# Feed-forward stages in groups of two f: four units' high products, then their low products, then two down units

## Chip, cores and metric

The kernel runs on one core of a Trainium2 chip. The metric is the device time of one execution in microseconds (us), the median of several runs. Lower is better.

## What is computed

The reference is four transformer blocks in a row on 256 tokens of width 1024, all in fp32. Each block has two SwiGLU feed-forward halves, so there are eight of them in all:

```python
def swiglu_ffn(x, wi, wo):
    g, u = jnp.split(x @ wi, 2, axis=-1)
    return (jax.nn.silu(g) * u) @ wo
...
x = x + 0.5 * swiglu_ffn(rmsnorm(x, ffn1_norm[i]), ffn1_wi[i], ffn1_wo[i])
```

The inner width is 2816, which is 22 slices of 128; a slice is called f. Between the feed-forward halves lie mixers (a chunked recurrence and windowed attention in the first two blocks; convolution, pooling and differential attention in the last two) and, in the first two blocks, a gate. The change doesn't touch these.

## The kernel before

**Weights.** All weights stream once through the core in units of 128 x 1024 fp32 (512 KB). SyncE loads unit u into one of four raw buffers as soon as the low part of unit u-4 is done. ScalarE then writes the high part of the unit, rounded to fp32r (`split` of `scalar`, L1190; it waits until the unit that had the slot before has been used up), and VectorE the low part, raw minus high (`split` of `vector`, L1821). High and low part of a unit share one of five slots (`W_SLOTS`), handed out to whichever was used longest ago (`placed_units`, L309). `step(s, k)` on ScalarE and VectorE makes the parts of the unit that lies three places ahead of place k of the stage (`lead`, L334; in the two feed-forward stages ahead of a `mixer2` the lead grows by one at each of k = 48, 51 and 54, as more slots are lent).

**A feed-forward stage** has 66 units, in the order of `ffn_order` (L60): two gate-and-up units per f (`gu`, each with half of the 1024 inputs), and one down unit per f (`o`). Each `gu` unit has eight high products with 512 columns (`gate_up_high`, L499: weights' high part against high and low part of x, side by side) and eight low products with 256 columns (`gate_up_low`, L518: weights' low part against x's high part). A slice uses two PSUM banks, 4 and 5 or 6 and 7 in turn. The order is two high units, their two low parts, one down unit (that of f-3), and so on. A down unit has twelve products of 512 columns (`unit_job`, L402).

**Between gate and down.** VectorE sums the halves of both banks (`summed`, L1956, two reductions), scales (`gated`, L1966), ScalarE applies Silu, VectorE multiplies (`product`, L1972), ScalarE rounds to the high part (`high_h`, L1261), VectorE subtracts (`low_h`, L1980). A down unit waits for `low_h` of its f. ScalarE and VectorE work through their instructions in program order, so these small operations stand in one queue with the splits.

**Stage ends.** The last two down units are worked together in `tail` (L451), by four blocks of the output; ahead of the last block TensorE transposes the first half of the new x (`turn_x`, L437). Those transposes wait for the first two additions of `into_x` (L1937) on VectorE, which stand in VectorE's queue behind the splits of the next stage's first units. In the very last stage `end_tail` (L472) works the last three down units together. At a stage's start `rest` transposes the other half of x.

Of the kernel before, what the change touches and what calls it, by code (L numbers as in the profile page):

```python
# [14 lines left out]
P = 128  # L15
# [29 lines left out]
TURNED_STEPS = ((0, 6), (8, 6))  # L45
# [108 lines left out]
def program(nc, d, out):  # L154
    ctx = ExitStack()
    with ctx:
# [237 lines left out]
        def tensor(pe, w):  # L394
# [103 lines left out]
            def ffn(s, n, m, u0):  # L498
# [52 lines left out]
                for k, (kind, f, half) in enumerate(ffn_order()):  # L551
# [3 lines left out]
                    if k == 6 and n != 11:  # L555
                        turn_r()
# [7 lines left out]
                    if kind == "gu":  # L564
                        gate_up_high(u, f, half)
                        if (n, k) == (11, 6):
# [617 lines left out]
        def scalar(act, w):  # L1184
# [70 lines left out]
            def ffn(s, i, n, m, u0):  # L1255
# [9 lines left out]
                order = ffn_order()  # L1265
                for k, (kind, f, half) in enumerate(order):
                    u = u0 + k
                    if u > 0 and (n, k) not in TURNED_STEPS:
                        step(s, k)
                    if k == 1 and n:  # L1270
                        rest(n)
                    if k == 2 and n in (0, 11):
                        squares(n)
                    if (n, k) == (0, 5):
                        w.wait_ge(*at("brow"))
                        copy(bias_row, pb[0][0:8, 0:384]).then_inc(*up("brow_out"))
                    if k == 6:
                        w.wait_ge(*at("rt", n))
                        copy(sbuf_h[:, 0, 1, :], pb[3][:, 0:S]).then_inc(*up("rrow", n))
                        for g in range(3):  # L1280
                            silu(g)
                        for g in range(2):
                            high_h(g)
                        if (n, k) in TURNED_STEPS:
                            step(s, k)
                    elif k > 6 and order[k - 1][2] == 1:
                        g = order[k - 1][1]
                        silu(g)
                        if g == NF - 1:
                            high_h(g)  # L1290
                        if g == 12 and n == 8:
                            w.wait_ge(*at("windows"))
                            copy(Pg[:, :, :, :], part2("tap").rearrange("p (g s t) -> p g s t", g=4, s=2)).then_inc(*up("Pg"))
                        if g == 4 and n in (2, 6):
                            w.wait_ge(*at("pin", i))
                            copy(PTh[:, :, :], pin).then_inc(*up("ph", i))
                    elif k > 6 and order[k - 2][2] == 1 and order[k - 2][1] < NF - 1:
                        high_h(order[k - 2][1])
# [487 lines left out]
            split(2)  # L1786
            for c in range(4, 8):
                high_x(0, c)
            split(3)
# [30 lines left out]
        def vector(dve, w):  # L1820
# [132 lines left out]
            def ffn(s, i, n, m, u0):  # L1953
                r_rows = sbuf_h[:, 0, 1, :]

                def summed(f):  # L1956

                    b = 4 + 2 * (f % 2)
                    w.wait_ge(*at("used", u0 + order.index(("gu", f, 1))))
# [25 lines left out]
                order = ffn_order()  # L1985
                for k, (kind, f, half) in enumerate(order):
                    u = u0 + k
                    if (n, k) in ((11, 2), (0, 2), (0, 3)):
                        summed(f)
# [1163 lines left out]
```

## Time and profile before

| | |
|---|---|
| median of 3 runs | 2049.31 us (2049.3 to 2049.9) |
| profiled execution: its own time | 2048.94 us |
| span of its trace | 2047.1 us |
| TensorE busy (matmuls) | 2038.7 us, 100% of the span |
| VectorE busy | 1488.5 us, 73% |
| ScalarE busy | 1097.2 us, 54% |
| HBM read | 375.73 MB, 184 GB/s |
| mean granted TensorE clock | 0.999 |

PE is TensorE's matmuls, PEld its weight loads, DVE VectorE, ACT ScalarE. In a timeline each row has the start in us, the time from start to end in us, the engine, the line, the operation, what it writes and reads, the shape and how many instructions were merged; in brackets the idle time before it and who ended that. Ends of matmuls are modelled and they overlap, so the pace of TensorE is read from start to start. L1188 is ScalarE's `copy`, used for splits (128x1024) and for `high_h` (128x256) alike.

### The profile page before, as it was taken

To read this page: it belongs to the slowest core of one execution; us is meant where nothing else is said; L and a number is where in the kernel's file an instruction comes from. 1 tells how busy PE (TensorE), PEld (TensorE's weight loads), DVE (VectorE), ACT (ScalarE), POOL (GpSimd) and SP (SyncE) were. 2 spreads that over 40 slices of the span, in tenths; PEclk is the share of its full clock that TensorE was granted. 3 is DMA by queue.
4 is the path that set the end of the run, shared out by engine and by line. 5 is a ranking of instruction groups with operands and counts; after the bars stand their busy time and mean duration, and the time that the engine had idled before them with its cause. 6 is when DMAs were issued, how large, how long until landed. Compare 5 with 4: busy or idle time off the path is not lost.

```text
span 2047.1 us, 27834 instructions
## 1 busy us (share of the span) xinstructions
PE 2038.7 (100%) x10803; PEld 1744.2 (85%) x10803; DVE 1488.5 (73%) x2240; ACT 1097.2 (54%) x1644; POOL 128.3 (6%) x140
## 2 busy tenths in 40 slices
PE   9999999999999999999999999999999999999998
PEld 8888888888888888888888888888888888888887
DVE  7776677777777767777777777788767777788766
ACT  5444664544554456655445545685445545685444
POOL 1000100000000001000000000160000000160000
PEclk9999999999999999999999999999999999999999
DMA  8654545555555555455555756425565656525553
GB/s 260 198 189 163 195 154 199 185 187 186 189 192 189 185 174 176 154 195 196 190 186 183 250 184 224 167 94 198 193 195 188 204 194 215 167 94 198 192 193 126
DMA packets 105539, 378.82 MB, mean 185 GB/s; under 512 B 12173, under 2 KB 12837, under 8 KB 105152
## 3 DMA queue, kind: packets, MB, share of 16 engines
q1 hardware_dynamic: 102224, 368.16, 53.9%
q0 software_dynamic: 2208, 7.71, 1.2%
q8 instruction: 86, 1.41, 0.3%
q10 hardware_dynamic: 976, 1.17, 0.2%
q14 instruction: 45, 0.37, 0.1%
HBM read 375.73 MB, written 1.27 MB: 184 GB/s over the span
## 4 chain that ended last, share of the span: by engine, by line
PE 99%; DVE 0%; DMA 0%; issue 0%; ACT 0%; ACTq 0%; POOLq 0%; POOL 0%
PE pb L516 31%; PE pb L527 16%; PE pb L415 15%; PE pb L416 14%; PE pb L420 14%; PE pb L586 1%; PE pb L443 1%; PE pb L463 1%; PE pb L465 1%; PE pb L464 1%; PE pb L989 0%; PE pb L650 0%; DMA X<-in_x 0%; PE pb L679 0%; PE pb L1030 0%
## 5 line engine op out<-in xcount | busy, mean ns | idle before, releaser
L1188 ACT ACTIVATE whi<-raw 128x1024 fp32r<-128x1024 f32 (+1 forms) x684 | 708.3, 1045 | 534.7 <-PE pb L527 421.1
L1827 DVE TENSOR_TENSOR wlo<-raw,whi 128x1024 fp32r<-128x1024 f32 (+1 forms) x680 | 821.8, 1217 | 46.9 <-ACT whi L1188 46.8
L516 PE MATMUL pb<-XT,whi 128*128 128x512 f32 x2784 | 665.8, 390 | 0.8 <-DVE XT L1842 0.5
L516 PEld LDWEIGHTS pb<-XT,whi 128*128 128x128 f32 x2784 | 519.6, 188 | 108.0 <-issue 1.5
L527 PEld LDWEIGHTS pb<-XT,wlo 128*128 128x128 f32 x2784 | 359.1, 191 | 14.9
L527 PE MATMUL pb<-XT,wlo 128*128 128x256 f32 x2784 | 363.9, 283 | 0.0
L1963 DVE TENSOR_REDUCE sbuf_s<-pb 128x256 f32<-128x512 f32 x240 | 154.6, 686 | 229.8 <-PE pb L527 229.8
L415 PE MATMUL pb<-whi,HTh 128*128 128x512 f32 x796 | 313.4, 394 | 0.1
L416 PE MATMUL pb<-whi,HTl 128*128 128x512 f32 x796 | 311.6, 391 | 0.0
L420 PE MATMUL pb<-wlo,HTh 128*128 128x512 f32 x796 | 302.1, 389 | 0.0
L420 PEld LDWEIGHTS pb<-wlo,HTh 128*128 128x128 f32 x796 | 149.5, 188 | 32.5
L415 PEld LDWEIGHTS pb<-whi,HTh 128*128 128x128 f32 x796 | 150.1, 189 | 26.9 <-issue 0.2
L416 PEld LDWEIGHTS pb<-whi,HTl 128*128 128x128 f32 x796 | 150.1, 189 | 24.9
L415 PE MATMUL pb<-whi,XT 128*128 128x512 f32 (+2 forms) x448 | 169.5, 382 | 0.0
L416 PE MATMUL pb<-whi,XT 128*128 128x512 f32 (+2 forms) x448 | 166.3, 375 | 0.0
L1963 DVE TENSOR_REDUCE sums<-pb 128x256 f32<-128x512 f32 x112 | 72.2, 686 | 127.9 <-PE pb L527 127.9
L2785 POOL TENSOR_TENSOR st<-st,cst 128x2 f32<-128x2 f32 (+3 forms) x35 | 49.8, 1423 | 1710.3 <-DVE st L1853 1516.2
L1259 ACT ACTIVATE sbuf_s<-sbuf_s 128x256 f32<-128x256 f32 x120 | 49.6, 419 | 168.4 <-DVE sbuf_s L1970 168.4
L420 PE MATMUL pb<-wlo,XT 128*128 128x512 f32 (+2 forms) x448 | 134.0, 375 | 0.0
L415 PEld LDWEIGHTS pb<-whi,XT 128*128 128x128 f32 x448 | 84.2, 188 | 16.3 <-issue 1.7
L416 PEld LDWEIGHTS pb<-whi,XT 128*128 128x128 f32 x448 | 84.4, 188 | 14.2
L420 PEld LDWEIGHTS pb<-wlo,XT 128*128 128x128 f32 x448 | 81.4, 188 | 15.4
(262 smaller groups left out, 1596.8 us busy)
## 6 DMA issues: line engine op xcount, KB each, us to landing
raw<-in_W SPq DMA_DIRECT2D x694, 512.0 KB, 4.2
raw<-in_W SPq DMA_DIRECT2D x8, 264.0 KB, 2.9
scr<-in_bc POOLq DMA_DIRECT2D x2, 640.0 KB, 5.1
raw<-in_W SPq DMA_DIRECT2D x4, 256.0 KB, 6.0
scr<-scratch POOLq DMA_DIRECT2D x8, 128.0 KB, 4.7
scr<-mrow POOLq DMA_DIRECT2D x2, 512.0 KB, 5.1
scr<-in_slope POOLq DMA_DIRECT2D x1, 1024.0 KB, 11.0
scr<-in_Pg POOLq DMA_DIRECT2D x1, 1024.0 KB, 14.2
```

Of the source, the lines that this page charges most:

```text
L415: pe.matmul(o, ah, bh, start=begin and i == 0, stop=False)
L416: pe.matmul(o, al, bh, start=False, stop=False)
L420: ins = pe.matmul(o, ah, bl, start=False, stop=end and i == len(parts) - 1)
L443: ins = pe.transpose(pb[b][:, t * P:(t + 1) * P], X[:, t, c * P:(c + 1) * P], ident[:, :])
L463: pe.matmul(o, ah, h[:, n * 512:n * 512 + 512], start=False, stop=False)
L516: pe.matmul(pb[b + j][:, :], h[:, k:k + P], xs, start=c == 0, stop=False)
L527: ins = pe.matmul(pb[b + j][:, 0:S], l[:, k:k + P], XT[:, c, 0, :], start=False, stop=c == KD - 1)
L1188: return act.activation(o, i, ACT.Copy, scale=scale)
L1259: act.activation(g, g, ACT.Silu).then_inc(*up("silu", s, f))
L1827: dve.tensor_tensor(low_w(u)[:, 0:c], raw[u % RAW_SLOTS][:, 0:c], high_w(u)[:, 0:c].bitcast(F32), ALU.subtract).then_inc(*up("lo", u))
L1963: dve.tensor_reduce(sums_of(f)[:, j, :], pb[b + j][:, :].rearrange("p (s t) -> p t s", s=2), AXX, ALU.add).then_inc(*up(name, s, f))
L2785: pool.tensor_tensor(r, v, cst[:, 0:1].to_broadcast([P, n]), ALU.pow).then_inc(*done)
```

## The change

A stage now goes in groups of two f. For f and f+1 the four `gu` units' high products come first, then their low products, then the down units of f-2 and f-1. The first four units do the same (their low products in the order 0, 2, 1, 3); for the last two f the low products follow after each f's two high units, as before. ScalarE's and VectorE's programs of the stage are written out anew for that order; the two exceptions named in `TURNED_STEPS` go. In the kernel's opening `split(2)` moves behind the four `high_x` (on VectorE `low_x`) calls. No work is added or left out.

```diff
 def ffn_order():
     order = [("gu", 0, 0), ("gu", 1, 0), ("gu", 0, 1), ("gu", 1, 1)]
-    for f in range(2, NF):
-        order += [("gu", f, 0), ("gu", f, 1)]
-        if f > 2:
-            order.append(("o", f - 3, 0))
-    return order + [("o", f, 0) for f in range(NF - 3, NF)]
+    for f in range(2, NF, 2):
+        order += [("gu", f, 0), ("gu", f, 1), ("gu", f + 1, 0), ("gu", f + 1, 1), ("o", f - 2, 0), ("o", f - 1, 0)]
+    return order + [("o", f, 0) for f in range(NF - 2, NF)]
+
+def low_products(k):
+    if k == 3:
+        return (0, 2, 1, 3)
+    kind, f, half = ffn_order()[k]
+    if k < 4 or kind == "o" or half == 0:
+        return ()
+    if f >= NF - 2:
+        return (k - 1, k)
+    return (k - 3, k - 2, k - 1, k) if f % 2 else ()
...
                         gate_up_high(u, f, half)
-                        if f < 2:
-                            gate_up_low(u, f, half)
-                        elif half == 1:
-                            gate_up_low(u - 1, f, 0)
-                            gate_up_low(u, f, 1)
+                        for q in low_products(k):
+                            _, g, part = order[q]
+                            gate_up_low(u0 + q, g, part)
...
 # ScalarE, one group
+                for f in range(2, NF - 2, 2):
+                    k = 3 * f - 2
+                    if f > 2:
+                        step(s, k)
+                        step(s, k + 1)
+                    step(s, k + 2)
+                    step(s, k + 3)
+                    silu(f)
...
+                    step(s, k + 4)
+                    silu(f + 1)
+                    high_h(f)
+                    if f == 12 and n == 8:
+                        w.wait_ge(*at("windows"))
+                        copy(Pg[:, :, :, :], part2("tap").rearrange("p (g s t) -> p g s t", g=4, s=2)).then_inc(*up("Pg"))
+                    step(s, k + 5)
+                    high_h(f + 1)
+                f = NF - 2
+                k = 3 * f - 2
+                step(s, k)
+                step(s, k + 1)
+                step(s, k + 2)
+                silu(f)
+                step(s, k + 3)
+                high_h(f)
+                step(s, k + 4)
+                silu(f + 1)
+                high_h(f + 1)
+                for q in range(k + 5, k + 8):
+                    step(s, q)
...
             split_half(1, 0)
             split_half(1, 1)
-            split(2)
             for c in range(4, 8):
                 high_x(0, c)
+            split(2)
             split(3)
...
 # VectorE, one group
+                for f in range(2, NF - 2, 2):
+                    k = 3 * f - 2
+                    if f > 2:
+                        step_and_lambda(k)
+                        low_h(f - 1)
+                        step_and_lambda(k + 1)
+                    step_and_lambda(k + 2)
+                    summed(f)
+                    step_and_lambda(k + 3)
+                    gated(f)
+                    summed(f + 1)
+                    step_and_lambda(k + 4)
+                    gated(f + 1)
+                    product(f)
...
+                    step_and_lambda(k + 5)
+                    product(f + 1)
+                    low_h(f)
+                f = NF - 2
+                k = 3 * f - 2
+                step(s, k)
+                low_h(f - 1)
+                step(s, k + 1)
+                summed(f)
+                step(s, k + 2)
+                gated(f)
+                step(s, k + 3)
+                product(f)
+                summed(f + 1)
+                gated(f + 1)
+                step(s, k + 4)
+                low_h(f)
+                product(f + 1)
+                low_h(f + 1)
+                for q in range(k + 5, k + 8):
+                    step(s, q)
```

## Rows read from the trace of the kernel before

**Rows 1.** The profile's page: span, TensorE's busy time, chain of work.
```profile
span 2047.1 us, 27834 instructions
...
PE 2038.7 (100%) x10803; PEld 1744.2 (85%) x10803; DVE 1488.5 (73%) x2240; ACT 1097.2 (54%) x1644; POOL 128.3 (6%) x140
...
PE 99%; DVE 0%; DMA 0%; issue 0%; ACT 0%; ACTq 0%; POOLq 0%; POOL 0%
```

**Rows 2.** Timeline of TensorE in the second feed-forward stage, one f and the next.
```profile
510.28 3.79 PE L516 MATMUL pb<-XT,whi 128*128 128x512 f32 x16
513.91 2.08 PE L527 MATMUL pb<-XT,wlo 128*128 128x256 f32 x16
515.82 0.40 PE L415 MATMUL pb<-whi,HTh 128*128 128x512 f32 x1
...
518.57 3.79 PE L516 MATMUL pb<-XT,whi 128*128 128x512 f32 x16
```

**Rows 3.** Timeline of VectorE and ScalarE in the same f.
```profile
515.12 1.06 ACT L1188 ACTIVATE whi<-raw 128x1024 fp32r<-128x1024 f32 x1 [2.89 <-PE pb L527]
...
516.02 1.29 DVE L1963 TENSOR_REDUCE sums<-pb 128x256 f32<-128x512 f32 x2 [2.53 <-PE pb L527]
517.23 0.41 DVE L1970 TENSOR_TENSOR sums<-sums,sbuf_h 128x256 f32<-128x256 f32 x1
517.56 1.22 DVE L1827 TENSOR_TENSOR wlo<-raw,whi 128x1024 fp32r<-128x1024 f32 x1
518.70 0.42 DVE L1977 TENSOR_TENSOR sbuf_h<-sums 128x256 f32<-128x256 f32 x1
...
517.68 0.42 ACT L1259 ACTIVATE sums<-sums 128x256 f32<-128x256 f32 x1 [1.49 <-DVE sums L1970]
518.00 1.04 ACT L1188 ACTIVATE whi<-raw 128x1024 fp32r<-128x1024 f32 x1
```

**Rows 4.** Timeline at the same stage's end: VectorE, ScalarE, then TensorE's tail and transposes.
```profile
526.98 0.42 DVE L1977 TENSOR_TENSOR sbuf_h<-sbuf_s 128x256 f32<-128x256 f32 x1
...
528.84 3.50 DVE L1827 TENSOR_TENSOR wlo<-raw,whi 128x1024 fp32r<-128x1024 f32 x3 [0.52 <-ACT whi L1188]
532.25 1.41 DVE L1842 SCALAR_TENSOR_TENSOR X<-pb,st,X 128x512 f32<-128x512 f32 x2
...
527.43 0.42 ACT L1188 ACTIVATE HTh<-sbuf_h 128x256 fp32r<-128x256 f32 x1 [1.05 <-DVE sbuf_h L1977]
527.76 3.14 ACT L1188 ACTIVATE whi<-raw 128x1024 fp32r<-128x1024 f32 x3
...
529.58 0.39 PE L463 MATMUL pb<-whi,HTh 128*128 128x512 f32 x1
...
533.66 1.03 PE L443 MATMUL pb<-ident,X 128*128 128x128 f32 x8
```

**Rows 5.** Timeline of the kernel's opening: TensorE, then ScalarE.
```profile
10.17 1.11 PE L527 MATMUL pb<-XT,wlo 128*128 128x256 f32 x8
11.12 1.09 PE L516 MATMUL pb<-XT,whi 128*128 128x512 f32 x4
12.05 1.03 PE L443 MATMUL pb<-ident,X 128*128 128x128 f32 x8
...
13.85 1.10 PE L527 MATMUL pb<-XT,wlo 128*128 128x256 f32 x8
...
11.33 1.06 ACT L1188 ACTIVATE whi<-raw 128x1024 fp32r<-128x1024 f32 x1 [0.64 <-DMA raw<-in_W]
12.47 1.57 ACT L1188 ACTIVATE XT<-pb,gcol 128x256 fp32r<-128x256 f32 x4
```

**Rows 6.** Timeline at the start of the stage behind the second gate (n = 8).
```profile
1120.94 1.98 PE L516 MATMUL pb<-XT,whi 128*128 128x512 f32 x8
...
1122.59 0.69 DVE L2472 TENSOR_TENSOR X<-X,scr 128x512 f32<-128x512 f32 x1
```

**Rows 7.** Timeline of ScalarE: the one copy of `Pg`, in the stage n = 8.
```profile
1221.06 1.90 ACT L1188 ACTIVATE Pg<-scr 128x2048 fp32r<-128x2048 f32 x1
```

More of the change, by code:

```diff
@@ L549, in end_ready @@
                     w.wait_ge(*at("hl", s, NF - 3 + i))
-                for k, (kind, f, half) in enumerate(ffn_order()):
+                order = ffn_order()
+                for k, (kind, f, half) in enumerate(order):
                     u = u0 + k
@@ L554, in ffn @@
                         rest(n)
-                    if k == 6 and n != 11:
+                    if k == 7 and n != 11:
                         turn_r()
@@ L1263, in high_h @@
                     copy(HTh[:, f % H_SLOTS, :], sbuf_h[:, f % 2, 0, :]).then_inc(*up("hh", s, f))
[L1265 to L1268, printed above, removed]
-                        step(s, k)
[L1270 to L1298, printed above, removed]
@@ new lines, in ffn @@
+                if u0:
+                    step(s, 0)
+                step(s, 1)
+                if n:
+                    rest(n)
+                if n in (0, 11):
+                    squares(n)
+                for k in range(2, 6):
+                    step(s, k)
+                if n == 0:
+                    w.wait_ge(*at("brow"))
+                    copy(bias_row, pb[0][0:8, 0:384]).then_inc(*up("brow_out"))
+                w.wait_ge(*at("rt", n))
+                copy(sbuf_h[:, 0, 1, :], pb[3][:, 0:S]).then_inc(*up("rrow", n))
@@ L1958, in summed @@
                     b = 4 + 2 * (f % 2)
-                    w.wait_ge(*at("used", u0 + order.index(("gu", f, 1))))
+                    w.wait_ge(*at("used", u0 + ffn_order().index(("gu", f, 1))))
                     if f > 2:
@@ L2033, in ffn, with step_and_lambda @@
+                def step_and_lambda(k):
+                    step(s, k)
                     if n in (8, 11) and k == 30:
@@ L2036, in ffn @@
                         lam_sum(i)
+                if u0:
+                    step(s, 0)
+                step(s, 1)
+                if n:
+                    rest(n)
+                summed(0)
+                if n in (0, 11):
+                    mean_x(n)
+                step(s, 2)
+                summed(1)
+                step(s, 3)
+                step(s, 4)
+                w.wait_ge(*at("r", n))
+                dve.tensor_copy(sbuf_h[:, 1, 1, :].rearrange("p (t e) -> p t e", t=2),
+                                r_of(n).unsqueeze(2).to_broadcast([P, 2, P])).then_inc(*up("rcopy", n))
@@ new lines, in ffn @@
+                dve.tensor_scalar(half_r(n), r_of(n), 0.5, None, ALU.mult).then_inc(*up("hr", n))
+                step(s, 5)
+                gated(0)
+                gated(1)
+                product(0)
+                product(1)
+                low_h(0)
+                low_h(1)
+                for f in range(2, NF - 2, 2):
[12 more added lines that the diff above has]
+                    product(f)
+                    if f == 4 and n in (2, 6):
+                        w.wait_ge(*at("ph", i))
+                        dve.tensor_tensor(PTl[:, :, :], pin, PTh[:, :, :].bitcast(F32), ALU.subtract).then_inc(
+                            *up("pl", i))
+                    step_and_lambda(k + 5)
+                    product(f + 1)
+                    low_h(f)
@@ new lines, in ffn @@
+                f = NF - 2
+                k = 3 * f - 2
+                step(s, k)
+                low_h(f - 1)
[13 more added lines that the diff above has]
+                    step(s, q)
@@ L2037, in ffn @@
+                u = u0 + len(ffn_order()) - 1
                 w.wait_ge(*at("hr", n))
@@ L2745, in vector @@
             split_half(1, 1)
-            split(2)
             for c in range(4, 8):
                 low_x(0, c)
+            split(2)
             split(3)
```

58 lines of the change are left out of this document (8 added, 50 removed).

## The prediction

> **What bounds the kernel now.** I read the page first: TensorE is busy for 2038.7 of 2047.1 us, and the chain that ended last is TensorE for 99% [rows 1]. So only two things can move the time: the pace of the matmuls, or pauses of TensorE that are there now or come new.
>
> For the pace I read TensorE's timeline in the middle of a feed-forward stage [rows 2]. From 510.28 to 513.91 it does 16 high products, 3.63 us or 227 ns each; to 515.82 16 low ones, 1.91 us or 119 ns each; to 518.57 the 12 products of a down unit, 2.75 us or 229 ns each. One f takes 8.29 us, with no pause: each change from one kind to the next comes at the pace of the kind that ends. In units: H (high products of one unit) 1.815, L (low) 0.955, O (down) 2.755.
>
> Then I read what the other two engines do in that time [rows 3]. ScalarE's split begins at 515.12, 1.21 us after the L that frees its slot began, having waited 2.89 us for it; VectorE's sums begin at 516.02, 2.11 us after the first L, having waited 2.53 us. Neither engine is late for anything. From start to start VectorE takes 1.21 for a pair of sums, 0.33 for a small operation and 1.14 for a split; ScalarE 0.32 for a Silu. A handover between them costs 0.04 (gated ends at 517.64, Silu starts at 517.68), a split of ScalarE 1.05, or 0.95 where the next instruction is ready.
>
> **The change, part by part.** The number of matmuls, splits, sums and loads stays the same, so the edit is worth nothing on TensorE by itself. Switches between high and low products become fewer, and a switch costs nothing now [rows 2]. What it can do is make TensorE wait.
>
> *A group in steady run.* TensorE's group is 4 H, 4 L, 2 O: 7.26 + 3.82 + 5.51 = 16.59, twice 8.29. Count from its first H and call its units 0 to 5. Slots come free in a burst: unit 0's at 7.26 + 1.21 = 8.47 for ScalarE, then 9.43, 10.38, 11.34. With five slots, unit 5 goes into the slot of unit 0, unit 6 into that of unit 1, and so on; so a chain through the two queues starts at 8.47. In program order: split 5, 8.47 to 9.52; its low part on VectorE, 9.56 to 10.70; sums of f to 11.91; low part 6 to 13.05; gated 13.47; Silu 13.50 to 13.82; split 7 to 14.87; low part 7, 14.91 to 16.05; gated of f+1 to 16.38; product of f to 16.80; its high part 16.83 to 17.15; split 8 to 18.20; low part 8, 18.24 to 19.38; product of f+1 to 19.80; its high part to 20.15; split 9 to 21.20. Unit 9 is the fourth H of the next group and is wanted at 16.59 + 5.45 = 22.03. So it comes 0.8 ahead. The others are earlier still (unit 8: 18.20 against 20.22; the down units and the high and low parts of f by several us). In steady run I take zero pauses, with 0.8 us of cover; the cover is gone if the chain of 12.7 us is 7% longer.
>
> *A stage's end.* Here the chain's lateness counts. The last group's program goes H H L L H H L L O O tail, with the tail at 16.59 again. ScalarE comes out of the group before at 20.15 - 16.59 = 3.57. Then: splits 61, 62, 63 to 4.62, 5.57, 6.52; VectorE low part 61, 4.66 to 5.80; low of f = 19 to 6.13; low part 62 to 7.27; sums of f = 20 to 8.48; low part 63 to 9.62; gated 10.04; Silu to 10.39; split 64 to 11.44; low part 64, 11.48 to 12.62; product 20 to 13.04; sums of f = 21, 12.96 to 14.17; gated 14.50; low part 65 to 15.64; low of 20 to 15.98 (done 16.06); product 21, 15.98 to 16.40. Before, that last product stood at 526.98, 2.60 ahead of the tail at 529.58 [rows 4]; now 0.6 ahead. Behind it in program order stand its high part, three splits on ScalarE (the next stage's first units), their three low parts on VectorE, and then the two additions into x. Before, these additions ran from 532.25 to 533.66, and TensorE's transposes began at 533.66: no slack at all [rows 4]. By the same steps they now run from 21.26 to 22.67, which is 4.67 behind the tail's start and not 2.67. So TensorE stands before the transposes, 2.0 us per stage end. (The low part of f = 21, done at 17.30, makes a pause of 0.1 in the tail, which is inside the 2.0.) The cost is read from no row directly: its lower bound is 0, if VectorE comes to the additions in time; the upper 3.1, with one more split in the chain. I take 2.0, since each step is a row.
>
> That upper case is the rule in the two stages ahead of the last mixers: there the lead grows at k = 54, which puts one split more into the group f = 18, and all that follows comes 1.14 later (one low part). 3.1 each. In the very last stage nothing is queued behind, but `end_tail` wants the low part of f = 20 at 11.08 + 2.755 + 1.36 = 15.2 and gets it at 16.06: 0.9.
>
> *The kernel's opening.* TensorE's second unit may start at 10.17 now, when the first H ends, and takes the same 2.73 (11.12 to 13.85, with eight transposes) [rows 5]: done at 12.90. The third H wants split 2. ScalarE's four `high_x` follow the transposes by 0.42 (12.05 to 12.47), so they now start near 11.5 and take 1.57; split 2, which ran ahead of them at 11.33, then ends at 14.05 [rows 5]. A pause of 1.2 that the low products used to fill. From 0 (if split 2 came first again) to 1.5.
>
> *Stages behind a gate* (n = 4 and 8). The second half of x is complete at 1123.28 [rows 6]. The transposes that want it come one H after the stage's start now, 1122.75, and not an H and an L after it: 0.5, and 0.1 for the first of them to be split. 0.6 each, 0 to 0.8. Other stages' additions end earlier; zero.
>
> *The copy of Pg.* It takes 1.90 [rows 7] and stands now ahead of split 8 in the chain: 0.8 of cover goes, 1.1 is a pause. Before it had TensorE's slack. 0 to 1.9.
>
> Sum: five stage ends at 2.0 are 10.0; two at 3.1 are 6.2; the last 0.9; opening 1.2; gates 1.2; Pg 1.1. Together 20.6. The profiled execution took 2048.94 with a span of 2047.1; 2048.94 + 20.6 = 2069.5. The median lies 0.4 above that execution, so 2070 us.
>
> **The rivals.** *One: the steady chain doesn't fit.* If handovers cost more than 0.04 where several waits meet, all 9 hand-overs from group to group in 8 stages pause. The point is 0.8 us more on the chain; at 0.3 us beyond it the price is 72 x 0.3 = 22, so 2092. For: the chain crosses the engines twelve times. Against: rows 3 show these crossings with their waits, at 0.04.
>
> *Two, not slower: the additions are in time.* At seven stage ends VectorE reaches the additions within 2.7 us of the tail's start, as now. This decides if the chain out of the group before is 2 us shorter than I have it, for instance if splits 61 to 63 run early. Then 16.2 and the 0.9 drop out, and 2070 becomes 2053, which is within 0.2%. For it: nothing is recomputed, both engines have idle time. Against: program order holds each split behind a Silu or a high part.
>
> *Three, faster: longer batches run at a better pace.* Eight low products take 0.95 (10.17 to 11.12), 16 take 1.91: 119 ns each in both [rows 5, 2]. Reading to 0.01 us, doubling the batch can save at most some 1 ns each; on 2816 low products that is 3 us, so even without any pause 2046. The Trainium skill (Perfetto Trace Analysis, Matmul Optimizations) says that TensorE scales power with its utilization and that it is therefore important to run matmuls back-to-back in batches. By that rule this change is a gain; the rows bear none of it out, as they stand back-to-back now.
>
> **How the numbers follow.** Forecast 0.65; rival one 0.18; two 0.13; three 0.04. A measurement of this kernel can tell 0.2%, 4 us, from no change. Faster by more than that: rival three with luck, 0.03. Within: rival two and the rest of three, 0.10, as half an us more at some stage end carries rival two out. Slower: 0.87. The range: the forecast's own terms run from 2060 (stage ends at 1.0, opening and gates at half) to 2082 (all stage ends at 3.1, Pg 1.9). Towards rival two I go to 2055, towards rival one to 2090; beyond them lie some 2 in 10.
>
> **What would show it.** Right: TensorE without pause from group to group; at each stage end the transposes (L443) begin 2 us later after the tail's first product (L463) than the 4.08 us of now [rows 4], named as waiting for VectorE's L1842; the third H of the opening waiting for ScalarE's split. Wrong: a pause ahead of every fourth H, named as ScalarE's split; or transposes in time at the stage ends; or another pace than 227 and 119 ns.

## The result, and the profile after

The changed kernel takes 2069.8 us (median of four runs, 2069.19 to 2070.36); the kernel before took 2049.61 us beside it (2049.3 to 2049.92). The ratio is 1.0098, 95% interval 1.0086 to 1.011: 20.2 us slower. The forecast was 2070. The profiled execution took 2070.36 us with a span of 2068.5, 21.4 above the span of before.

The page of the changed kernel, which answers to [rows 1]. In it L525 are the high products, L536 the low ones, L424, L425 and L429 the down units, L472 to L474 the tail, L452 transposes of x, L489 `end_tail`; L1196 is ScalarE's copy, L1851 VectorE's low parts, L1866 among others its additions into x.

```profile
span 2068.5 us, 27833 instructions
...
PE 2043.0 (99%) x10803; PEld 1741.5 (84%) x10803; DVE 1492.7 (72%) x2240; ACT 1085.4 (52%) x1644; POOL 127.1 (6%) x140
...
PE 89%; DVE 6%; ACT 3%; issue 2%; DMA 1%; SPq 0%; POOLq 0%; POOL 0%; ACTq 0%; DVEq 0%
```

TensorE does the same 10803 products, and the chain that ended last was TensorE's for 99% of the span; now it is for 89%, and VectorE and ScalarE stand in it with 9%. So it is no longer only its own pace that TensorE follows. For whom it waits, the view of its waits tells (what waited, for whom: us in total, times, longest):

```profile
PE pb L452 <- DVE X L1866: 9.3, 14, 1.1
PE pb L525 <- ACT whi L1196: 2.5, 3, 1.0
PE pb L472 <- DVE HTl L2006: 2.4, 4, 1.0
PE pb L525 <- DVE XT L1866: 1.8, 2, 1.1
...
PE pb L489 <- DVE HTl L2006: 0.8, 1, 0.8
```

The first line is the stage ends: 14 waits, two at each of seven ends, of transposes for the additions into x. One of these ends, that of the second feed-forward stage, in the timeline: TensorE, then VectorE, then ScalarE. It answers to [rows 4].

```profile
533.24 0.39 PE L472 MATMUL pb<-whi,HTh 128*128 128x512 f32 x1
...
537.28 0.39 PE L474 MATMUL pb<-whi,HTl 128*128 128x512 f32 x1
538.75 0.30 PE L452 MATMUL pb<-ident,X 128*128 128x128 f32 x1 [1.08 <-DVE X L1866]
539.32 0.98 PE L452 MATMUL pb<-ident,X 128*128 128x128 f32 x7 [0.27 <-DVE X L1866]
...
528.12 1.23 DVE L1851 TENSOR_TENSOR wlo<-raw,whi 128x1024 fp32r<-128x1024 f32 x1 [1.43 <-ACT whi L1196]
...
532.60 0.41 DVE L2001 TENSOR_TENSOR sbuf_h<-sbuf_s 128x256 f32<-128x256 f32 x1
...
534.44 3.50 DVE L1851 TENSOR_TENSOR wlo<-raw,whi 128x1024 fp32r<-128x1024 f32 x3 [0.52 <-ACT whi L1196]
537.86 2.06 DVE L1866 SCALAR_TENSOR_TENSOR X<-pb,st,X 128x512 f32<-128x512 f32 x3
...
526.72 0.42 ACT L1267 ACTIVATE sums<-sums 128x256 f32<-128x256 f32 x1 [3.53 <-DVE sums L1994]
527.04 1.04 ACT L1196 ACTIVATE whi<-raw 128x1024 fp32r<-128x1024 f32 x1
```

The additions begin at 537.86, 4.62 behind the tail's first product at 533.24; before, it was 532.25 - 529.58 = 2.67. The transposes follow with two pauses. Further up stands where VectorE lost time: from 526.69 to 528.12 it did nothing, since the next thing in its program is the low part of a unit whose high part ScalarE makes only after Silu (526.72, then the split at 527.04).

Below, n numbers the parts of the program in order: the feed-forward stages are n = 0, 2, 4, 6, 8, 10, 11 and 13; a gate stands ahead of n = 4 and 8, a `mixer2` behind n = 8 and 11. An end with neither a `mixer2` nor the kernel's end behind it (n = 0, 2, 4, 6, 10) is called a plain end. Laying both traces over each other at the same products of TensorE, the lag of the changed kernel grows like this (us):

| place | predicted | measured |
|---|---|---|
| opening (first stage up to its tail) | 1.2 | 1.85 |
| five plain stage ends | 5 x 2.0 | 1.95, 1.95, 1.96, 1.96, 1.94 |
| gate ahead of n = 4 | 0.6 | 0.59 |
| n = 8: gate, Pg, end | 0.6 + 1.1 + 3.1 = 4.8 | 5.21 |
| n = 11: a pause, end | 3.1 | 3.72 |
| last stage: its `end_tail` | 0.9 | 1.07 |
| steady run of the stages n = 2, 6, 10 and 13, and the mixers | 0 | -0.73 |
| sum | 20.6 | 21.5 |

### The profile page after: what moved, and what is told of

Read it like the earlier page. It is cut to its first block, busy times and chain, and to the rows that moved or that the text cites. A ratio compares the mean times of both kernels' runs of the same rounds, so it can differ in the third digit from the quotient of the medians.

```text
span 2068.5 us, 27833 instructions
## 1 busy us (share of the span) xinstructions
PE 2043.0 (99%) x10803; PEld 1741.5 (84%) x10803; DVE 1492.7 (72%) x2240; ACT 1085.4 (52%) x1644; POOL 127.1 (6%) x140
## 3 DMA queue, kind: packets, MB, share of 16 engines
q10 hardware_dynamic: 976, 1.17, 0.2%
## 4 chain that ended last, share of the span: by engine, by line
PE 89%; DVE 6%; ACT 3%; issue 2%; DMA 1%; SPq 0%; POOLq 0%; POOL 0%; ACTq 0%; DVEq 0%
PE pb L525 29%; PE pb L536 15%; PE pb L424 13%; PE pb L425 13%; PE pb L429 13%; DVE wlo L1851 2%; ACT whi L1196 2%; PE pb L594 1%; PE pb L452 1%; DMA raw<-in_W 1%; DVE sbuf_s L1987 1%; PE pb L474 1%; PE pb L472 1%; PE pb L473 1%; DVE X L1866 0%
## 5 line engine op out<-in xcount | busy, mean ns | idle before, releaser
L1851 DVE TENSOR_TENSOR wlo<-raw,whi 128x1024 fp32r<-128x1024 f32 (+1 forms) x680 | 820.9, 1216 | 384.9 <-ACT whi L1196 384.7
L1196 ACT ACTIVATE whi<-raw 128x1024 fp32r<-128x1024 f32 (+1 forms) x684 | 692.2, 1044 | 310.9 <-PE pb L536 202.3
L525 PE MATMUL pb<-XT,whi 128*128 128x512 f32 x2768 | 650.0, 390 | 4.4 <-ACT whi L1196 2.5
L525 PEld LDWEIGHTS pb<-XT,whi 128*128 128x128 f32 x2768 | 516.8, 188 | 114.1 <-ACT whi L1196 6.6
L536 PEld LDWEIGHTS pb<-XT,wlo 128*128 128x128 f32 x2768 | 344.4, 191 | 7.2
L536 PE MATMUL pb<-XT,wlo 128*128 128x256 f32 x2768 | 347.1, 283 | 0.0
L424 PE MATMUL pb<-whi,HTh 128*128 128x512 f32 x804 | 315.6, 392 | 0.0
L425 PE MATMUL pb<-whi,HTl 128*128 128x512 f32 x804 | 313.9, 390 | 0.0
L429 PE MATMUL pb<-wlo,HTh 128*128 128x512 f32 x804 | 305.2, 389 | 0.0
L429 PEld LDWEIGHTS pb<-wlo,HTh 128*128 128x128 f32 x804 | 151.0, 188 | 32.2
L424 PEld LDWEIGHTS pb<-whi,HTh 128*128 128x128 f32 x804 | 151.3, 188 | 28.8
L425 PEld LDWEIGHTS pb<-whi,HTl 128*128 128x128 f32 x804 | 151.3, 188 | 27.8
L424 PE MATMUL pb<-whi,XT 128*128 128x512 f32 (+2 forms) x448 | 169.6, 382 | 0.0
L425 PE MATMUL pb<-whi,XT 128*128 128x512 f32 (+2 forms) x448 | 166.2, 375 | 0.0
L1196 ACT ACTIVATE HTh<-sbuf_h 128x256 fp32r<-128x256 f32 x176 | 73.3, 418 | 143.3 <-DVE sbuf_h L2001 143.3
L429 PE MATMUL pb<-wlo,XT 128*128 128x512 f32 (+2 forms) x448 | 134.0, 375 | 0.0
L424 PEld LDWEIGHTS pb<-whi,XT 128*128 128x128 f32 x448 | 84.2, 188 | 16.3 <-issue 1.7
L1267 ACT ACTIVATE sums<-sums 128x256 f32<-128x256 f32 x56 | 23.5, 419 | 139.1 <-DVE sums L1994 139.1
L425 PEld LDWEIGHTS pb<-whi,XT 128*128 128x128 f32 x448 | 84.4, 188 | 14.2
```

The costliest lines, as they stand in the source:

```text
L424: pe.matmul(o, ah, bh, start=begin and i == 0, stop=False)
L425: pe.matmul(o, al, bh, start=False, stop=False)
L429: ins = pe.matmul(o, ah, bl, start=False, stop=end and i == len(parts) - 1)
L525: pe.matmul(pb[b + j][:, :], h[:, k:k + P], xs, start=c == 0, stop=False)
L536: ins = pe.matmul(pb[b + j][:, 0:S], l[:, k:k + P], XT[:, c, 0, :], start=False, stop=c == KD - 1)
L1196: return act.activation(o, i, ACT.Copy, scale=scale)
```

## The experiments

Each undoes a part, adds a known load, or changes one order. Line numbers shift by a few between kernels. "Lag" is counted as in the table.

**Is there really no slack at a stage's end?** Kernel before, with two subtractions of 128x512 (0.69 us each) into a scrap tile on VectorE, ahead of the last low part of each stage; nothing reads the scrap.

```diff
             def step(s, k):
                 for u in split_at(s, k):
+                    if stages[s][0] == "ffn" and k == 65 and u < n_units:
+                        w.wait_ge(*at("hi", u))
+                        for cut in (slice(0, 512), slice(512, 1024)):
...
+                            dve.tensor_tensor(pad[:, :], raw[u % RAW_SLOTS][:, cut], high_w(u)[:, cut].bitcast(F32),
+                                              ALU.subtract).then_inc(*up("pad", s, cut.start))
                     split(u)
```

> The kernel before, with two further subtractions of 128 x 512 on VectorE (into a scrap tile; some 1.3 us together) ahead of the last low part at each of seven stage ends. Theory (no slack between the additions and the transposes): each end grows by 1.3, 2049.5 + 9 = 2058.5. Rival (the transposes were in time with room to spare, and the pause of the changed kernel has another cause): 2049.5 to 2051.

Measured: 2058.49 us (ratio 1.0045, 1.0029 to 1.0062). Two of them, back to back, take 1.33 from start to start (532.25 to 533.58); the lag over an end is 1.24 to 1.34 at six of the seven (1.87 at n = 11). All of it reaches the end: no slack, as the prediction read from [rows 4]. VectorE, then TensorE's tail, at the end of the second stage:

```profile
532.25 1.41 DVE L1848 TENSOR_TENSOR pad<-raw,whi 128x512 bf16<-128x512 f32 x2
533.58 1.22 DVE L1828 TENSOR_TENSOR wlo<-raw,whi 128x1024 fp32r<-128x1024 f32 x1
534.72 1.40 DVE L1853 SCALAR_TENSOR_TENSOR X<-pb,st,X 128x512 f32<-128x512 f32 x2
...
530.72 0.39 PE L464 MATMUL pb<-whi,HTh 128*128 128x512 f32 x1
```

**Does the steady chain have its 0.8 us of cover?** Changed kernel with scrap copies on ScalarE, right ahead of the split that stands behind Silu of f, in each group from f = 4 on; in one kernel one copy of 128x512 (0.61 us), in the other two of 128x1024 (1.05 us each).

```diff
                     silu(f)
...
+                    for j in range(1 if f > 2 else 0):
+                        w.wait_ge(*at("ss", *in_junk[-1]))
+                        in_junk.append((n, "pad", (f, j)))
+                        copy(junk[:, 0:512], X[:, 0, 0:512]).then_inc(*up("ss", *in_junk[-1]))
                     step(s, k + 4)
```

> The changed kernel with one further ScalarE copy of 128 x 512 (into a scrap tile, some 0.6 us) ahead of the Silu of f+1 in each group from f = 4 on, so that the chain through the two queues is 0.6 longer. Theory (0.8 us of cover in steady run, none at the stage ends): no pause from group to group, 0.5 to 0.6 more at each of eight ends, 2074. Rival (the steady chain has no cover): 56 further pauses of 0.5, 2098 or more.

> As before, with two copies of 128 x 1024, some 2.0 us on the chain. Theory (0.8 us of cover): a pause of 1.2 ahead of the fourth high unit of 56 groups, 67 us, and 2.0 at each of eight ends, 16 us: 2153. Rival (the chain doesn't bind, TensorE's lead is larger): as the six tenths of the shorter one, stage ends alone, 2086.

Measured: 2076.93 us (ratio 1.0134) with the small copy, 2173.89 us (a single execution) with the two large ones. TensorE's waits for splits, first of the kernel with one copy, then of the one with two:

```profile
PE pb L525 <- ACT whi L1196: 3.5, 5, 1.0
```
```profile
PE pb L525 <- ACT whi L1196: 50.1, 61, 1.8
```

With 0.6 us more the high products wait for splits at 5 places only (3 in the changed kernel), and between 480 and 520 us TensorE has no pause at all. By the starts of the products one group in n = 2 and one in n = 6 has its fourth high unit 0.28 us late, which this view doesn't list; in the group before it ScalarE has one more copy of 128x512 (`PTh`, 0.61 us), so that there the chain is longer by both. With 2.1 more they wait at 61 places: from group to group. So the cover lies between these two, as worked out.

Both kernels came out slower than expected, by 3 and by 21 us, and the starts of the products tell where. With the small copy the five plain ends cost 0.53 more each, as expected; what came on top stands in the groups of n = 2 and 6 (0.41 each), n = 8 (0.97) and n = 11 (0.31), and at the end of n = 11 (0.7). With the large ones the fourth high unit of a group begins 17.97 behind that of the group before, in place of 16.55. That is 1.42 for each such group, near the 2.1 - 0.8 = 1.3 of the sum, so beyond its cover the chain costs what it overhangs; 56 of them make 80 us, where the expectation took 1.2 each, 67. The plain ends cost 2.05 more each, as expected, but those of n = 8, n = 11 and the last stage 3.7, 4.3 and 4.8. Why these three cost more is not shown.

**Is it the place of the additions in VectorE's queue?** Changed kernel with the first two additions ahead of the last two low parts.

```diff
-                for q in range(k + 5, k + 8):
-                    step(s, q)
+                step(s, k + 5)
...
+                def last_splits():
+                    step(s, k + 6)
+                    step(s, k + 7)
+
+                into_x(u, [hr[:, t:t + 1] for t in range(2)], m, last_splits)
```

> The changed kernel, but at each stage end VectorE makes the first two additions into x ahead of the low parts of the last two of the next stage's first three units, not behind them. Theory (TensorE stands because VectorE's queue reaches the additions late): the additions start about 2.4 us behind the tail's first product and not 4.6, the transposes come in time, and 1.7 us go at each of seven ends: 2069.8 - 11.8 = 2058. Rival (the late product of the last f, not the place of the additions, holds the end, or the additions wait for TensorE's own blocks): the transposes stay late, 2067 to 2070.

Measured: 2064.31 us (ratio 1.0072), 6 off the expectation. The wait of the transposes for the additions (L1866) is gone from the list, but other waits came. The list, then VectorE at the end of the second stage, where the tail's first product begins at 532.22:

```profile
PE pb L424 <- DVE XT L1866: 2.5, 4, 0.6
PE pb L525 <- DVE XT L1866: 2.1, 3, 1.0
```
```profile
534.58 1.54 DVE L1866 SCALAR_TENSOR_TENSOR X<-pb,st,X 128x512 f32<-128x512 f32 x2
536.04 2.35 DVE L1851 TENSOR_TENSOR wlo<-raw,whi 128x1024 fp32r<-128x1024 f32 x2
```

The first two additions are in time, 2.36 behind the tail. But the two low parts that were passed now stand ahead of the remaining additions and of what follows from them, and the next stage's first products wait instead. A plain end cost 0.75 or 1.37 in place of 1.95. So VectorE's queue as a whole is late there, and this order of its last steps passes part of the lateness on; the expectation had left that out.

**Opening and gates.** Changed kernel with the low products of the first four units of each stage right behind their high ones, as before.

```diff
 def low_products(k):
-    if k == 3:
-        return (0, 2, 1, 3)
+    if k < 4:
+        return (k,)
     kind, f, half = ffn_order()[k]
-    if k < 4 or kind == "o" or half == 0:
+    if kind == "o" or half == 0:
         return ()
```

> The changed kernel, but the first four units of each stage have their low products right behind their high ones, as in the kernel before. Theory (in the opening and behind a gate TensorE runs through its high products and then waits for x or a split; low products in between fill that wait): 1.2 goes in the opening and 0.6 at each of two gates: 2069.8 - 2.4 = 2067.4. Rival (the opening waits for its loads whatever the order): 2069 or more.

Measured: 2068.33 us. Against the changed kernel the opening gives back 1.68 us and the two gates 0.72 and 0.65: at these three places the low products had lain over a wait, as the prediction says. But n = 11 became 0.89 slower and the end of n = 0 by 0.27, so the order that the change gave the first four units is the better one there; what waits in those two places I did not follow.

**Pg and the last stage.** Changed kernel with the copy of `Pg` ahead of Silu of its group, and `low_h` of f = 20 ahead of `gated` of f = 21. ScalarE first, then VectorE:

```diff
                     step(s, k + 3)
+                    if f == 12 and n == 8:
+                        w.wait_ge(*at("windows"))
+                        copy(Pg[:, :, :, :], part2("tap").rearrange("p (g s t) -> p g s t", g=4, s=2)).then_inc(*up("Pg"))
                     silu(f)
...
                 summed(f + 1)
+                low_h(f)
                 gated(f + 1)
                 step(s, k + 4)
-                low_h(f)
                 product(f + 1)
```

> The changed kernel with two moves that are apart in time: ScalarE's copy of Pg goes ahead of the Silu of its group, where ScalarE idles 3 us, and at a stage's end the low part of h of f = 20 comes ahead of the last f's scaling. Theory: the pause of 1.0 in the group f = 14 of n = 8 goes, and that of 0.95 in the very last stage: 2069.8 - 1.9 = 2067.9; the other stage ends stay as they are. Rival (these pauses belong to the order of the products, not to two places in the queues): 2069.8.

Measured: 2067.91 us. The sum came out as expected, its parts did not. The stage n = 8 up to its tail gained 2.26 us and n = 11 gained 1.18, the ends of n = 0, 8 and 11 lost 0.64, 0.94 and 0.64, and the last stage kept 0.92 of its 1.07. Of the 2.26 at n = 8, 1.17 lie before the stage's last high product and are the copy of `Pg`, near the 1.1 predicted. The other 1.09 lie right ahead of the tail, like the 1.18 of n = 11, where there is no copy: in the changed kernel the tail waits there for `low_h` (L472 in the list of waits above). The early `low_h` ends that wait but makes VectorE's additions later, 6.03 and 5.64 behind the tail at these two ends in place of 5.03, and it doesn't cure the last stage's pause (the splits do, below).

**All three together.** The three edits above in one kernel.

> The changed kernel with the three edits together: additions ahead of the last two splits, low products right behind the high ones in each stage's first four units, and the copy of Pg and the low part of f = 20 moved up. TensorE's groups of four, four and two stay. Theory (all that the change costs lies in places of the two queues, none in the grouping): 11.8 + 2.4 + 1.9 go, 2053.7; what stays is 1.2 in each of the two tails ahead of the last mixers and 0.8 in n = 11. Rival (the grouping has a price of its own): 2058 or more.

Measured: 2061.51 us (ratio 1.0057), 8 above the expectation. By its number alone the rival of that run, a price of the grouped order itself, would hold. What it left was waits by name (those of the first edit above, and two in the tails, 2.2 us), so the next theory was about who makes VectorE late.

**Who makes VectorE late?** The rows of the stage end say: VectorE stood 1.43 us before a low part whose split was queued on ScalarE behind Silu, which itself waited 3.53 for VectorE. Three kernels from the changed one, VectorE's program being left as it was in the first two. One moves these splits ahead of Silu and the high parts in all groups (and the copy of `Pg` behind Silu of f), the next in the last group alone:

```diff
                     step(s, k + 2)
                     step(s, k + 3)
+                    step(s, k + 4)
+                    step(s, k + 5)
                     silu(f)
...
-                    step(s, k + 4)
                     silu(f + 1)
                     high_h(f)
...
-                    step(s, k + 5)
                     high_h(f + 1)
                 f = NF - 2
...
                 step(s, k + 2)
-                silu(f)
                 step(s, k + 3)
-                high_h(f)
+                silu(f)
                 step(s, k + 4)
+                high_h(f)
                 silu(f + 1)
```

The third has beside these the low products behind the high ones in the first four units of n = 0, 4 and 8 only, and the early `low_h` of f = 20.

```diff
-def low_products(k):
+def low_products(k, n):
+    if k < 4 and n in (0, 4, 8):
+        return (k,)
     if k == 3:
         return (0, 2, 1, 3)
```

> The changed kernel with another order on ScalarE alone: in every steady group the last two splits stand ahead of Silu of f (the copy of Pg behind that Silu), and in the last group the two splits that stood behind Silu and the first high part stand ahead of them. VectorE's program is as it was. The theory says that the lateness at the stage ends grows where VectorE stands 1.43 us before a split that is queued behind Silu or a high part: then the pauses of 2.0 us at five ends and of 3.4 at two, the 0.95 in the last stage, the 1.0 of Pg and the 0.8 of n = 11 go, and 2050 to 2051 us are left (opening 1.7 and two gates at 0.6, less 0.14 in each of eight stages). The rival, that VectorE's own queue of low parts, sums and products is too long for this order whatever ScalarE does, gives 2060 us or more.

> The changed kernel with ScalarE's order changed in the last group of each stage alone (two splits ahead of Silu and the first high part). If the waits of VectorE for splits in that last group make the lateness, 1.43 us go at each of seven ends and 0.95 in the last stage: 2059 us. If the group before it has made it already, about as the changed kernel, 2068 to 2070 us.

> As the kernel with the splits ahead, and beside it the low products of a stage's first four units right behind the high ones in the stages n = 0, 4 and 8 alone (the opening and the two behind a gate), and low of f = 20 ahead of its neighbour's scaling. If opening and gates are then as in the kernel before, 1.7 and 1.2 us more go: 2048.5 to 2049.5 us, level with the kernel before or up to 1 us under it. The rival, that the grouped order keeps a price of its own, gives 2052 us or more.

Measured: 2052.77 us with the splits ahead everywhere (ratio 1.0013, 1.0004 to 1.0023), 2057.93 with them ahead in the last group alone (1.0038, 1.0024 to 1.0052), 2049.9 with the two repairs (1.0000, 0.9991 to 1.0009), which is 0.4 above its expectation. The order of a few instructions on ScalarE, in the last group alone, takes back 12 of 20 us. A plain end gives back 1.5 of its 1.95; at the two ends ahead of a `mixer2` the additions still begin 4.82 and 4.12 behind the tail. With the splits ahead everywhere the pauses of the last stage and of n = 11 are gone too. TensorE's waits, splits ahead everywhere; the transposes' wait of 9.3 us for the additions (L1866) is no longer among them:

```profile
PE pb L525 <- DVE XT L1866: 1.4, 2, 1.1
PE pb L525 <- ACT whi L1196: 1.0, 1, 1.0
PE pb L1172 <- POOL sbuf_s L2965: 1.0, 1, 1.0
PE pb L452 <- DVE X L2514: 0.6, 2, 0.3
```

The kernel with the splits ahead everywhere came out 2 us above the expectation, because the ends were not quite in time: 0.33 to 0.35 at each of five, 0.29 and 0.17 at the two ahead of a mixer2, 2.2 in sum. VectorE and TensorE at the end of the second stage, first of this kernel, then of the one with the splits ahead in the last group alone:

```profile
529.46 0.42 DVE L2001 TENSOR_TENSOR sbuf_h<-sbuf_s 128x256 f32<-128x256 f32 x1
...
534.73 2.06 DVE L1866 SCALAR_TENSOR_TENSOR X<-pb,st,X 128x512 f32<-128x512 f32 x3
...
531.72 0.39 PE L472 MATMUL pb<-whi,HTh 128*128 128x512 f32 x1
...
535.80 1.37 PE L452 MATMUL pb<-ident,X 128*128 128x128 f32 x8
536.92 0.47 PE L472 MATMUL pb<-whi,HTh 128*128 128x512 f32 x1
```
```profile
534.46 2.06 DVE L1866 SCALAR_TENSOR_TENSOR X<-pb,st,X 128x512 f32<-128x512 f32 x3
...
531.35 0.39 PE L472 MATMUL pb<-whi,HTh 128*128 128x512 f32 x1
```

With the splits ahead everywhere the additions begin 3.01 behind the tail, 0.34 more than before's 2.67, and the transposes take 1.12 to the next product, where they took 0.79 before (533.66 to 534.45).

**A version at or under the kernel before.** The last of these kernels with two moves on VectorE in the last group: the last product (of f = 21) goes ahead of the low part that stood before it, and `low_h` of f = 20 goes back behind `gated`, where the changed kernel has it. The expectation names the first move alone; what each of the two is worth is not shown.

```diff
                 summed(f + 1)
-                low_h(f)
                 gated(f + 1)
-                step(s, k + 4)
+                low_h(f)
                 product(f + 1)
+                step(s, k + 4)
                 low_h(f + 1)
```

> As the kernel with the splits ahead and the two small repairs, and beside it VectorE's last product (of f = 21) ahead of the low part that stood before it in the last group. The trace of that kernel still has its additions 0.3 to 0.4 us later behind the tail than the kernel before, at each of five ends, and 0.1 to 0.2 at the two ahead of a mixer2. If the additions are in time now, these 2.1 us go and only the gain of 0.14 us in each stage is left: 2047.6 to 2048.3 us, some 0.08% under the kernel before. If TensorE's pauses there have another cause, 2049.9 us as without it.

Measured: 2047.76 us against 2049.55 of before beside it, ratio 0.9991 (0.9982 to 1.0000); the span is 2045.6 against 2047.1. The grouped order, with its queues in the right order, is not slower, and by this measure 0.09% faster, at the edge of what the interval can tell. At the end of the second stage:

```profile
532.19 1.40 DVE L1868 SCALAR_TENSOR_TENSOR X<-pb,st,X 128x512 f32<-128x512 f32 x2
...
529.69 0.39 PE L474 MATMUL pb<-whi,HTh 128*128 128x512 f32 x1
...
533.78 1.03 PE L454 MATMUL pb<-ident,X 128*128 128x128 f32 x8
534.57 0.48 PE L474 MATMUL pb<-whi,HTh 128*128 128x512 f32 x1
```

Five kernels agree in what an end costs. For the end of n = 2, where "late" is the start of the additions behind the tail's first product, less the 2.67 of before:

| kernel | additions behind tail | late | lag gained over the end |
|---|---|---|---|
| before, with two subtractions | 534.72 - 530.72 = 4.00 | 1.33 | 1.30 |
| changed | 537.86 - 533.24 = 4.62 | 1.95 | 1.95 |
| splits ahead in the last group | 534.46 - 531.35 = 3.11 | 0.44 | 0.45 |
| splits ahead everywhere | 534.73 - 531.72 = 3.01 | 0.34 | 0.33 |
| and the last product ahead | 532.19 - 529.69 = 2.50 | -0.17 | 0.01 |

The kernel with the additions ahead stands outside this: there they come 2.36 behind the tail, in time, and this end still costs 0.75, for the work that they passed.

**What is the small gain in the steady stages?** The stages n = 2, 6, 10 and 13 (up to its `end_tail`) became 0.14 us shorter, which the prediction didn't have. Start to start, the first five wide products (512 columns) behind low ones take 233, 236, 228, 232 and 231 ns, all others 226.7 (means of 18 units in the second stage of before; the same in the changed kernel). That is 27 ns for each such change. The first low products behind wide ones take 113 and 119 ns in place of 120: 7 ns back. My first thought was VectorE's sums, which read the banks just then. To tell the two apart, a kernel from before with the low products of each unit right behind its own high ones:

```diff
-                        if f < 2:
-                            gate_up_low(u, f, half)
-                        elif half == 1:
-                            gate_up_low(u - 1, f, 0)
-                            gate_up_low(u, f, 1)
+                        gate_up_low(u, f, half)
```

> The kernel before with the low products of every gate-and-up unit right behind its own high ones: two changes from high to low and two from low to wider products for each f, in place of one and one. Same products, same work of the other engines. If the first five wide products behind low ones cost 27 ns in sum, and the change from wide to low gives 7 ns back, as the start-to-start times of TensorE's rows say, 20 ns come on top for each of 20 f in 8 stages: 3.2 us, 2052.9 us. The rival is that those products are slow since VectorE's sums read the banks beside them: then nothing is added, 2049.7 us.

Measured: 2052.54 us (ratio 1.0015, 1.0006 to 1.0023). The timeline of TensorE, one f:

```profile
486.27 1.98 PE L516 MATMUL pb<-XT,whi 128*128 128x512 f32 x8
488.09 1.11 PE L527 MATMUL pb<-XT,wlo 128*128 128x256 f32 x8
489.04 2.00 PE L516 MATMUL pb<-XT,whi 128*128 128x512 f32 x8
490.88 1.11 PE L527 MATMUL pb<-XT,wlo 128*128 128x256 f32 x8
491.83 0.40 PE L415 MATMUL pb<-whi,HTh 128*128 128x512 f32 x1
```

Eight high products behind a down unit take 1.82 (486.27 to 488.09), behind low ones 1.84 (489.04 to 490.88), with no sums beside them. Each steady stage became 0.40 us longer, which is 20 times 20 ns. The change of kind is the cause; VectorE's sums are not. In the changed kernel 18 f in nine groups have nine such changes fewer, 0.18 us at 20 ns; the stage gained 0.14, and what takes the rest is not shown.

## Why the prediction was right

*The number.* 2070 against 2069.8 is closer than the working deserves. In the profiled executions the lag is 21.5 and not 20.6, and the terms missed by 0.65 (opening), 1.2 (the ends ahead of a `mixer2`, Pg and the last stage), -0.24 (the plain ends) and -0.73 (steady run and mixers). That these nearly cancel is luck; the mechanism at the stage ends, 10 of the 20 us, is not. The upper end of the forecast's own terms was added wrongly: eight ends at 3.1, 1.9 for Pg, 1.5 for the opening and 1.6 for the gates make 2079, not 2082, which changes nothing in the range.

*What bounds the kernel.* Right. Nothing was added to or taken from TensorE's work, and all that was lost is pauses.

*A group in steady run.* Right in its result and in its steps. The sum put the split of the next group's fourth unit at 20.15 to 21.20 behind the group's first high product. In the trace ScalarE reaches it, after the high part of f+1, like this (ScalarE, then on TensorE the low products of the group that wants the unit):

```profile
486.81 0.42 ACT L1196 ACTIVATE HTh<-sbuf_h 128x256 fp32r<-128x256 f32 x1 [1.62 <-DVE sbuf_h L2001]
487.14 1.99 ACT L1196 ACTIVATE whi<-raw 128x1024 fp32r<-128x1024 f32 x2
...
490.81 4.00 PE L536 MATMUL pb<-XT,wlo 128*128 128x256 f32 x32
```

The group that wants this unit has its low products at 490.81 and so began 7.26 earlier, at 483.55; its fourth unit is wanted 5.45 later, at 489.00. The split began at 487.14, and at 1.04 it ends at 488.18, with 0.8 to spare. Rival one, the chain that doesn't fit, fell: it needed 0.8 us more, and the kernel with 0.6 us more still ran from group to group without pauses, but for those groups where ScalarE had another copy to make.

*A stage's end.* Right: 1.94 to 1.96 for each of the five, where the steps gave 2.0; the additions stood 4.62 behind the tail, where they gave 4.67. The sign that was named came in part: in the second stage the first of the eight transposes begins 5.51 behind the tail and the others 6.08, where before all began 4.08 behind it, so they are 1.43 and 2.0 later, and they wait for the additions (L1866, L1842 of before). Rival two, the additions in time, fell with this. Its condition, that the chain is shorter because splits run early, is what the kernel with the splits ahead everywhere then made nearly true by hand, and it landed where that rival put the time (2052.77; the rival said 2053). That the two numbers meet so closely is luck: the rival still had 1.1 for Pg, which was gone, and no pauses at the ends, where 2.2 was left. What the prediction named as the reason against it, "program order holds each split behind a Silu or a high part", was the cause of 17 of the 20 us (2069.8 to 2052.77, with the copy of `Pg` moved beside the splits). The Trainium skill (PSUM — Partial Sum Buffer, Engine vs sequencer instructions) calls the queues of ScalarE and VectorE strict FIFO; the row with 1.43 us of wait, at the head of VectorE's queue, is what that looks like here.

*The two ends ahead of a mixer2, Pg and the last stage.* Their sum was near: 10.0 against 8.8 (with the gate of n = 8). At n = 11 stands a pause that no step had:

```profile
1633.06 2.14 PE L525 MATMUL pb<-XT,whi 128*128 128x512 f32 x8 [0.62 <-ACT whi L1196]
```

It is a split late in an early group; it goes when the splits stand ahead, so it belongs to the same chain. I had worked out one group and taken it for all.

*The opening.* The pause was right in place and size; the term came out 0.65 larger for another reason. The timeline of TensorE, then of ScalarE, answers to [rows 5]:

```profile
12.62 1.17 PE L525 MATMUL pb<-XT,whi 128*128 128x512 f32 x4
14.81 3.92 PE L525 MATMUL pb<-XT,whi 128*128 128x512 f32 x16 [1.02 <-ACT whi L1196]
...
7.89 0.63 ACT L1196 ACTIVATE whi<-raw 128x512 fp32r<-128x512 f32 x1 [0.94 <-DMA raw<-in_W]
...
10.12 1.15 ACT L1196 ACTIVATE whi<-raw 128x512 fp32r<-128x512 f32 x2 [0.86 <-DMA raw<-in_W]
12.25 1.57 ACT L1196 ACTIVATE XT<-pb,gcol 128x256 fp32r<-128x256 f32 x4 [0.98 <-PE pb L452]
13.69 2.97 ACT L1196 ACTIVATE whi<-raw 128x1024 fp32r<-128x1024 f32 x3
```

The third high unit waits for the split behind the four `high_x`, as said. In before, the second unit's last four high products took 1.01 until the low ones began at 13.85 (they began at 12.84, and the low ones are the row of [rows 5]), so the second unit's end at 12.62 + 1.01 = 13.63 leaves a pause of 1.18 up to 14.81: the 1.2 of the sum. The rest came earlier, with the first loads: ScalarE waited for weights to land until 7.89 and 10.12, where before it began the same splits at 7.36 and 9.38. That differs from run to run: the first high product comes from 0.31 us sooner to 0.57 later than before in the kernels run here, and five others with the same opening lost between 1.33 and 1.93 in it.

*The gates.* Right: 0.59 at n = 4.

*Switches and rival three.* Here one sentence was wrong: that a change from one kind of product to the next costs nothing. It costs 20 ns for both directions. The prediction's own numbers had a sign of it: 229 ns for the twelve products of the down unit, which stand behind low ones, against 227 for the high ones (2.75 us, where twelve at 226.7 ns make 2.72). The prediction bounded the gain at 1 ns for each low product, 3 us; it was 0.14 us in a stage, some 1.1 us in all, 0.05%. The granted clock was 0.999 in both kernels. So of the reason that the Trainium skill gives for the rule under rival three (Perfetto Trace Analysis, Matmul Optimizations: TensorE scales power with its utilization, hence batches back to back) the traces here show nothing, and longer batches are a small gain by the fewer changes of kind. The order of ScalarE's queue was worth 17 us, fifteen times that.

## What to carry to other kernels

Where two engines hand small results to and fro, and transfers of bulk work (here the splits) stand in the same queues, write down the program order of both, and look for the instruction that could start long ago but stands behind one that waits: bulk work whose input is ready goes ahead of the small step that isn't. When a group of work is made larger, redo that order, above all for the last group of a stage, since the lateness that steady run hides comes due there. Before you move anything, find the place without slack (here the additions, 2.67 us behind the tail), and test any order by that number first. Then look whether the wait has only moved to what stands behind, as it did with the additions ahead.

## What the runs showed of the hardware

TensorE's pace depends a little on what came before: wide products (128x512) take 226.7 ns from start to start, but the first five behind narrow ones (128x256) 233, 236, 228, 232 and 231, and the first two narrow ones behind wide ones 113 and 119 in place of 120. It is the same in the five kernels where I took it, with and without reads of the banks beside it, and 160 more such changes cost 3 us of 2049.55. Kind and width change together in these kernels (weights' high or low part, 512 or 256 columns); which of the two it is, is not shown.
